# Retention on x without its norm, contiguous mixer weights, and routing tables moved out of two early places for down matrices

## The reference

```python
h = rmsnorm(x, norm_mix_g[0]);  x = x + retention_mixer(h, ...)      # layer 0
h = rmsnorm(x, norm_mix_g[1]);  x = x + conformer_conv_mixer(h, ...) # layer 1
# after each mixer: h = rmsnorm(x, norm_ffn_g[i]); x = x + hierarchical_moe(h, ...)
# retention, per head (4 heads, dk 256, dv 512):
q, k = rotary(h @ w_q), rotary(h @ w_k) * dk ** -0.5;  v = h @ w_v;  g = h @ w_g
o = causal_decayed(q, k) @ v
o = o * rsqrt(mean(o * o) + 1e-6) * head_g
out = (silu(g) * o) @ w_out
# moe: top-1 group of 4, top-2 of its 8 experts, blocks of tokens per expert:
y = (silu(xb @ w_gate[e]) * (xb @ w_up[e])) @ w_down[e]
```

## Time and profile before

| | us |
|---|---|
| median of 3 runs | 1786.35 (1784.78 to 1788.58) |
| the profiled execution | 1786.88 |
| its span | 1785.0 |
| TensorE matmuls, busy | 1471.5 (82%) |
| TensorE weight loads, busy | 936.2 (52%) |
| VectorE busy | 522.5 (29%) |
| ScalarE busy | 486.3 (27%) |
| GpSimd busy | 337.2 (19%) |
| moved by DMA | 473.19 MB, mean 265 GB/s |

### The profile page before, as it was taken

One profiled execution on the slowest core, in us unless ns is written; L12 is line 12 of the kernel. 1 busy time (PEld: TensorE's weight loads), 2 busy tenths in 40 slices (PEclk: granted clock), 3 DMA queues, 4 the chain that ended last, 5 costly groups with the idle time before them and its releaser, 6 DMA issues. The chain is left out here.

```text
span 1785.0 us, 37105 instructions
## 1 busy us (share of the span) xinstructions
PE 1471.5 (82%) x15156; PEld 936.2 (52%) x15157; DVE 522.5 (29%) x1245; ACT 486.3 (27%) x875; POOL 337.2 (19%) x294
## 2 busy tenths in 40 slices
PE   5999999999786889867785899869788878679883
PEld 4878678786443445434353785337344444345442
DVE  3222111212521112111123399961412111112124
ACT  4232422323321222211122324341322122112222
POOL 2424244342000111100011452012010001001100
PEclk8999999999798999999997899979799899999997
DMA  8222122121599999999998121004499999999985
GB/s 283 96 93 94 48 95 95 47 95 53 192 428 429 427 429 427 429 428 429 429 409 288 47 95 47 0 1 164 180 376 414 406 430 423 429 427 428 415 361 212
DMA packets 65156, 473.19 MB, mean 265 GB/s; under 512 B 6509, under 2 KB 23101, under 8 KB 39506
## 3 DMA queue, kind: packets, MB, share of 16 engines
q1 hardware_dynamic: 60064, 463.55, 63.4%
q0 software_dynamic: 4608, 8.41, 1.2%
q10 hardware_dynamic: 434, 0.51, 0.1%
HBM read 461.94 MB, written 14.68 MB: 267 GB/s over the span
## 5 line engine op out<-in xcount | busy, mean ns | idle before, releaser
L787 PE MATMUL ps<-ring,hgT 128*32 128x256 f32 x6016 | 385.3, 409 | 147.2 <-DMA ring<-w_gu 122.7
L787 PEld LDWEIGHTS ps<-ring,hgT 128*32 128x32 f32 x6016 | 202.5, 116 | 318.0 <-DMA ring<-w_gu 147.8
L431 POOL TENSOR_TENSOR w_lo<-ring,w_hi 128x512 fp32r<-128x512 f32 x176 | 233.0, 1326 | 415.1 <-ACT w_hi L511 415.1
L450 POOL DMA_INDIRECT y_dram<-area_c,idx_s x96 | 94.3, 982 | 788.6 <-ACT area_c L547 768.9
L511 ACT CAST w_hi<-ring 128x512 fp32r<-128x512 f32 x176 | 109.1, 625 | 367.1 <-PE ps L692 366.7
L730 PE MATMUL ps<-area_a,block_rows 128*32 128x256 f32 x3136 | 201.3, 400 | 8.9 <-DVE block_rows L976 8.9
L1098 DVE TENSOR_TENSOR a_e<-sg_e,ps 128x128 f32<-128x128 f32 x94 | 27.1, 288 | 613.3 <-ACT sg_e L542 613.3
L803 PE MATMUL ps<-ring,aT_e 128*32 128x256 f32 x2752 | 166.3, 382 | 23.6 <-DMA ring<-w_down 10.7
L730 PEld LDWEIGHTS ps<-area_a,block_rows 128*32 128x32 f32 x3136 | 110.3, 117 | 85.0 <-issue 26.6
L1237 DVE SCALAR_TENSOR_TENSOR area_c<-area_b,par,area_c 128x512 f32<-128x512 f32 x168 | 135.6, 878 | 1.1
L690 PE MATMUL ps<-w_hi,hT_hi 128*128 128x512 f32 x320 | 126.7, 396 | 7.2 <-DVE hT_lo L1262 7.2
(11 more groups left out here) (183 smaller groups left out, 1473.6 us busy)
## 6 DMA issues: line engine op xcount, KB each, us to landing
ring<-w_gu SPq DMA_DIRECT2D x128, 2048.0 KB
ring<-w_down SPq DMA_DIRECT2D x58, 2048.0 KB
ring<-w_in SPq DMA_DIRECT2D x8, 2048.0 KB
ring<-w_in SPq DMA_DIRECT2D x8, 1024.0 KB
ring<-w_out SPq DMA_DIRECT2D x4, 2048.0 KB
ring<-w_pw SPq DMA_DIRECT2D x8, 1024.0 KB
hT<-w_down SPq DMA_DIRECT2D x2, 2048.0 KB, 7.7
area_c<-w_down SPq DMA_DIRECT2D x2, 2048.0 KB, 8.0
```

Source lines behind the costliest of these rows:

```text
L431: nc.gpsimd.tensor_tensor(w_lo[:, place, :], ring[:, s, at:at + 512], w_hi[:, place, :].bitcast(F32), ALU.subtract).then_inc(lo_ready, 1)
L450: pool.indirect_dma_start(y_dram[l], bass.IndirectOffsetOnAxis(ap=idx_s[:, b:b + 1].bitcast(U32), axis=0), y_out[:, b, :], None, bounds_ch ...
L787: last = nc.tensor.matmul(ps[32 * g:32 * g + 32, 2, 0:256], hgT[:, n * (KT // 2) + k, :], gate_up[n][:, k, :, g * P:(g + 1) * P], start=(n ...
```

## The change

1. The norm before retention is no longer computed ahead of it. TensorE turns x itself as each tile lands. ScalarE squares x in the first head, between weight tiles 4 and 5, and the scales are applied to v, to the gate's SiLU, and to the epsilon of the head norm. The counters of later norms move down by one.
2. The mixer weights are laid out on the host as places of the ring, and each is one contiguous load of 2 MB. Router weights and biases are loaded by SyncE behind head 0's gate weights, positions behind its q and k weights. The clamps are on VectorE, and the sine is behind weight tile 8. ScalarE's four heads are written out without a loop.
3. The routing's tables move to area_c from column 4096 and to trig. The down matrices for area_c and area_b are loaded ahead of the routing: in layer 0 right behind the first two experts, in layer 1 when the conv mixer has left z (`hTlo_ready`). Since `y_out` is where the tables are, ScalarE waits for `wts_ready` before a layer's blocks.

```diff
-        onehot_r = over("onehot_r", [P, (NT * 2 + 1) * NE], area_b_at, 400)
-        slot_hot_r = over("slot_hot_r", [P, 8, P], area_c_at, 0)
-        block_hot_r = over("block_hot_r", [P, 8, NBLK], area_c_at, 8 * P)
+        route_at = 4096
+        onehot_r = over("onehot_r", [P, (NT * 2 + 1) * NE], area_c_at, route_at + 1152)
+        slot_hot_r = over("slot_hot_r", [P, 8, P], trig_at, 0)
+        block_hot_r = over("block_hot_r", [P, 8, NBLK], area_c_at, route_at)
...
-            sp.dma_start(area_b[:, 0:S].bitcast(I32), pos_in.partition_broadcast(P)).then_inc(pos_loaded, 16)
             sp.dma_start(const[:, :], const_in).then_inc(const_loaded, 16)
             for i in range(NT):
                 sp.dma_start(x[:, i, :], x_in[i * P:(i + 1) * P, :]).then_inc(x_loaded[i], 16)
-            load_head_qk(0)
-            load_columns(1, w_in, KT, 2 * QK, DV)
+            load_slot(0, w_qk[0])
+            sp.dma_start(area_b[:, 0:S].bitcast(I32), pos_in.partition_broadcast(P)).then_inc(pos_loaded, 16)
+            load_slot(1, w_v[0])
             sp.dma_start(decay[:, :, :], decay_in.rearrange("h p s -> p h s")).then_inc(decay_loaded, 16)
-            load_columns(2, w_in, KT, 2 * QK + RV, DV)
-            load_rows(3, w_out, 0, DV)
+            load_slot(2, w_g[0])
+            sp.dma_start(wr[:, :, :, :], w_router).then_inc(router_loaded, 16)
...
+            load_slot(3, w_out[0])
...
+                if l == 0:
+                    load_spare(1)
+                    load_spare(2)
+                sp.wait_ge(logitT_mm[l], 1)
+                load_spare(0)
                 sp.wait_ge(cum_ready[l], 1)
-                for n, left in enumerate((logitT_mm, idx_mm, wts_ready)):
-                    sp.wait_ge(left[l], 1)
-                    sp.dma_start(spare[n], w_down[l, SPARE[n]]) \
-                        .then_inc(spare_loaded[l][n], 16)
                 if l == 1:
+                    sp.wait_ge(idx_mm[l], 1)
                     sp.dma_start(gfin, g_final.partition_broadcast(P)).then_inc(gfin_loaded, 16)
...
-                        load_columns(j, w_pw1, KT, j * 2 * P, 2 * P)
-                        load_columns(j, w_pw1, KT, j * 2 * P + D, 2 * P, at=2 * P)
+                        load_slot(j, w_pw1[j])
...
+                    sp.wait_ge(hTlo_ready, 3 * KT)
+                    for n in (1, 2):
+                        sp.dma_start(spare[n], w_down[1, SPARE[n]]).then_inc(spare_loaded[1][n], 16)
                     sp.wait_ge(lo_ready, split + TILES)
-                    load_expert(0, w_gu0[1, 0])
+                    load_slot(0, w_gu0[1, 0])
...
-            pool.wait_ge(angle_ready, 1)
-            nc.gpsimd.tensor_scalar(sin, ang, PI, -PI, ALU.min, ALU.max).then_inc(trig_arg, 1)
-            nc.gpsimd.tensor_scalar(cos, low, PI, -PI, ALU.min, ALU.max).then_inc(trig_arg, 1)
...
                 total = act.value_load(cum[0:1, NE:NE + 1], min_val=NE, max_val=NBLK - 1)
+                act.wait_ge(wts_ready[l], 1)
                 with act.Fori(0, total) as t:
...
+            for h in range(HEADS):
...
+                split(0, 0, NWT)
+                if h == 0:
                     for i in range(NT):
+                        act.wait_ge(x_loaded[i], 16)
+                        link.sent(nc.scalar.activation(xn[:, i, :], x[:, i, :], ACT.Square,
+                                                       accum_out=x_ss[:, i:i + 1]))
+                    act.wait_ge(pad_zero, 1)
+                    link.wait()
+                    nc.scalar.activation(x_rt, x_ss, ACT.Sqrt, bias=eps, scale=1.0 / D).then_inc(x_root_ready, 1)
+                split(0, NWT, TILES)
+                if h == 0:
+                    act.wait_ge(trig_arg, 2)
+                    nc.scalar.activation(trig[:, :, :], trig[:, :, :], ACT.Sin).then_inc(trig_ready, 1)
...
+                    nc.scalar.activation(v[:, i, :], ps[:, B + i, :], ACT.Copy, scale=x_rstd2[:, i:i + 1]) \
+                        .then_inc(v_ready, 1)
...
+                    nc.scalar.activation(sg[:, i, :], ps[:, A + i, :], ACT.Silu, scale=x_rstd[:, i:i + 1]) \
+                        .then_inc(sg_ready, 1)
...
+                    nc.scalar.activation(rt[:, i:i + 1], ss[:, i:i + 1], ACT.Sqrt, bias=x_eps[:, i:i + 1],
+                                         scale=1.0 / DV).then_inc(oroot_ready, 1)
...
-            turn_norm(0)
+            for i in range(NT):
+                pe.wait_ge(x_loaded[i], 16)
+                for k in range(KT):
+                    last = nc.tensor.transpose(ps[:, k, i * P:(i + 1) * P], x[:, i, k * P:(k + 1) * P], ident)
+                    if i == NT - 1:
+                        last.then_inc(hT_mm, 1)
...
+            dve.wait_ge(par_loaded, 16)
+            norm_lo(0, 0, G_MIX)
+            V.sem_inc(x_added, 8)
             dve.wait_ge(const_loaded, 16)
...
+            dve.wait_ge(x_root_ready, 1)
+            link.done(V.reciprocal(x_rstd, x_rt))
+            V.tensor_scalar(x_eps, x_ss, EPS / D, EPS * EPS, ALU.mult, ALU.add)
+            V.tensor_tensor(x_rstd2, x_rstd, x_rstd, ALU.mult).then_inc(x_scale_ready, 1)
```

More of the change, by code:

```diff
@@ L89, in done, with program @@
         self.wait()
-def program(nc, x_in, pos_in, const_in, decay_in, par_in, w_in, w_out, w_pw1, w_pw2, b_pw2,
+def program(nc, x_in, pos_in, const_in, decay_in, par_in, w_qk, w_v, w_g, w_out, w_pw1, w_pw2, b_pw2,
             w_router, b_router, w_gu0, w_gu1, w_down, g_final, out):
@@ L120, in program @@
         area_c = sb("area_c", [P, 6144])
+        trig_at = next_tensor()
         trig = sb("trig", [P, 2, S])
@@ L167, in program @@
         expert_exp = small[:, 16:20]
+        x_rstd, x_rstd2, x_eps, x_ss, x_rt = (small[:, n:n + 4] for n in range(20, 40, 4))
         xn = area_a[:, :].rearrange("p (i d) -> p i d", i=NT)
@@ L189, in program @@
                  hT[:, 0:4, :].rearrange("p k s -> p (k s)"), hT[:, 4:8, :].rearrange("p k s -> p (k s)")]
[L192 to L202, removed]
+        room = area_c[:, route_at:route_at + GRP * QW]
+        logitsT = area_c[0:NG + NE, route_at:route_at + S]
+        logits = room[:, 512:656].rearrange("p (i e) -> p i e", i=NT)
+        le = room[:, 656:784].rearrange("p (i e) -> p i e", i=NT)
+        eq = room[:, 784:912].rearrange("p (i e) -> p i e", i=NT)
+        block_hot = room[:, 576:1152].rearrange("p (j b) -> p j b", j=8)
+        work = room[:, 1440:1696].rearrange("p (j e) -> p j e", j=8)
+        table = room[:, 1696:1696 + NBLK]
+        group_hot = room[:, 1768:1784].rearrange("p (i g) -> p i g", i=NT)
+        pick, best, second, gate = (room[:, 1784 + 4 * n:1788 + 4 * n] for n in range(4))
+        rank, base = room[:, 1800:1808], room[:, 1808:1816]
+        ranki, blki = room[:, 1816:1824].bitcast(I32), room[:, 1824:1832].bitcast(I32)
+        count, blocks, upto = room[:, 1832:1864].bitcast(I32), room[:, 1864:1896], room[:, 1896:1928]
         spare = [hT[:, :, :].rearrange("p k s -> p (k s)"), area_c[:, 0:SLOT], area_b[:, 0:SLOT]]
         gfin = trig[:, :, :].rearrange("p a s -> p (a s)")
-        block_hot = area_c[:, 3328:3328 + 8 * NBLK].rearrange("p (j b) -> p j b", j=8)
         y_out = area_c[:, 4096:4096 + GRP * QW].rearrange("p (b c) -> p b c", b=GRP)
@@ L217, in program @@
         par_loaded = sem("par_loaded")
+        router_loaded = sem("router_loaded")
         pos_loaded = sem("pos_loaded")
@@ L1276, in _ @@
             combine(1, 4)
-_NAMES = ("x_in", "pos_in", "const_in", "decay_in", "par_in", "w_in", "w_out", "w_pw1", "w_pw2", "b_pw2",
+_NAMES = ("x_in", "pos_in", "const_in", "decay_in", "par_in", "w_qk", "w_v", "w_g", "w_out", "w_pw1", "w_pw2", "b_pw2",
           "w_router", "b_router", "w_gu0", "w_gu1", "w_down", "g_final")
@@ L1320, with slots @@
                           columns(a["conv_ln_b"]), taps], axis=1)
+    w_in = a["ret_w_in"][0]
+    def slots(w):
+        n = w.shape[1]
+        return w.reshape(KT, P, n, 512).transpose(2, 1, 0, 3).reshape(n, P, SLOT)
     def tiled(w):
```

171 lines of the change are left out of this document (76 added, 95 removed).

## The result

The changed kernel took 1765.94 us (median of four runs, 1763.18 to 1768.34) against 1786.02 us for the kernel before in the same rounds: ratio 0.9886, 95% interval 0.9871 to 0.9902. The forecast was 1769.3 in a range of 1765 to 1777. A repeat of the changed kernel gave 1767.37 (ratio 0.9898, interval 0.9884 to 0.9912). The first median lies 0.9 us inside the forecast's lower edge, the repeat's 2.4. The profiled execution took 1768.34 us with a span of 1766.5, 18.5 us less than the profiled one of before.

A forecast was written before the change was run, and what follows sets the result against it. It took TensorE and ScalarE to bound the mixers and DMA the MoE layers. Terms 8.0 + 7.7 + 0 + 1.8 - 0.2 = 17.3 us gave 1769.6, or 1769.1 against the median; it said 1769.3, range 1765 to 1777.

The forecast's parts named there:

- Start: Kernel start: with the norm off the path and x landing earlier, the first mixer matmul comes 8.0 us earlier.
- the cover: First head: ready matmuls hide ScalarE's squares, root and table load before cast 5; cost nothing, 3 us without it.
- Rival (b): Start: bound by first weights or by a table load before hi copies; 3 to 4 us instead of 8; chance 0.12.
- Mixer: Retention mixer: scale operands cost nothing or hundredths of a microsecond, unrolled ScalarE heads 0, bounds -2 to +1 us.
- Rival (d): ScalarE's four unrolled heads must be fetched, at 80 instructions; 0.22 us each cancels the gain; chance 0.05.
- Stream of the first MoE layer: First MoE layer: spares load before the routing, so slot 0's refill meets an empty queue; 7.7 us earlier.
- rival (a): First MoE layer: stream's shift lost as TensorE becomes the bound near its end; gain left 9.6, 1777; chance 0.10.
- rival (e): Whole change: spares load when they did and x lands as late; about 1785; chance 0.02.
- Second layer: Second MoE layer: early spares bring forward a transfer already hidden; 0 us, bounds -0.3 and +0.3.
- The wait for the weights: Each MoE layer: ScalarE waits for VectorE's last weight before the first SiLU; 0.1 us each, bounds 0 and 1.3.
- Contiguous w_pw1: End of first MoE layer: contiguous conv weights finish before the last scatter; gain 1.8 us, bounds 0.3 and 2.3.
- rival (c): w_pw1 loads: 1 KB runs cost nothing, 352 GB/s comes from scatters beside; last term falls, 1771; chance 0.05.

The follow-up runs named there:

- router_front: Changed kernel with router weights, biases and positions loaded ahead of x again; 1769.33 us, ratio 0.991.
- norm_kept2: Kernel before, norm kept, with contiguous mixer weights and first loads ordered positions, x, then router weights; 1780.65 us, ratio 0.9973.
- norm_kept: Kernel before, norm kept, with contiguous mixer weights and the changed kernel's order of first loads (positions behind w_qk); 1790.74 us, ratio 1.003.
- preload: Changed kernel plus a four-element ScalarE copy ahead of its first wait on data, bringing in the hi copies' table; 1767.13 us, ratio 0.9895.
- dve_order: Changed kernel with the angles ahead of the low parts of x in VectorE's program; 1777.69 us, ratio 0.9957.
- tables: Kernel before with only the third part: routing tables moved, two spare down matrices loaded early, new wait for routing weights; 1777.65 us, ratio 0.9955.
- late0: Changed kernel with layer 0's down matrices for area_c and area_b loaded behind the routing again; 1772.41 us, ratio 0.9929.
- late1: Changed kernel with layer 1's down matrices for area_c and area_b loaded behind the routing again; 1767.03 us, ratio 0.9895.
- best: Changed kernel with an early four-element ScalarE table-load copy and the wts_ready wait moved to the first y_out write; 1766.85 us, ratio 0.9895.
- pw1_strided: Changed kernel with w_pw1 loaded by eight strided loads with 1 KB runs again; 1766.21 us, ratio 0.989.

## Why the prediction was right, and where its steps were off

**Start: 8.0 forecast, 8.64 at the first matmul.** That the sum came out is in part luck, since two of its steps were wrong by nearly the same amount and in opposite directions. By the prediction: x 1.5 us earlier, norm chain 5.66, table load 1.28, in all 8.4. By the trace: x 8.95 - 5.59 = 3.36 earlier, norm chain 5.66 as forecast, transposes to hi copies 7.28 instead of 5.46 (-1.82), hi copies to the first matmul 6.65 instead of 8.09 (+1.44). The first failed term is the rate: 0.58 MB left the queue and gave 3.36 us, or 173 GB/s, where I had assumed at least the 297 GB/s of a full window. `router_front` gives the same price (3.7 us), and positions alone explain most of it: x lands at 8.01 with them ahead (`norm_kept2`) and at 5.68 without (`norm_kept`), 2.3 us for 256 KB. The second is the stretch before the hi copies: 1.29 of the 1.82 is the table load, which I took as gone, and 0.53 the transposes, which take 6.66 us instead of 6.13. I had looked only at the place where the load stood. In the kernel before, the last work ahead of the hi copies was the sine, which brought in its table in the shadow of the transposes, and the copies ran with that:

```profile
17.13 1.28 ACT L562 ACT_TABLE_LOAD   x1
```

With the norm and the sine both moved away, the copies are ScalarE's first work and need a load of their own. I had the case as a bound (1.3 us); `preload` shows that it was this bound that held. Cast 5 started at 25.40, right behind ScalarE's own chain and 5.9 us after the first matmul instead of 5.4, with TensorE busy throughout: the cover held. Rival (b) falls in its first half: the weights had landed by 15.42 at the latest (`preload`). Its second half, the table load, came true and cost its 1.3 us, but not the start. The 8.64 is one pair of executions: with this start unchanged, the first matmul stood at 19.02 to 19.52 in five executions, and with that of before at 27.58 and 28.16, so the gain lies between 8.1 and 9.1. And the order of VectorE's program, which the prediction did not name as a condition, is one: `dve_order` and `norm_kept` lost 10.1 and 8.1 us at the first matmul by it.

**Mixer: 0 forecast, -0.3.** SiLU with a scale operand takes 2.42 us for four instead of 2.07, between products that did not move. Rival (d), straight code that has to be fetched, needed 0.22 us at each of 80 places to cancel the gain, 17.6 in all; the whole mixer lost 0.34, and even that is within what it varies by: 424.5 to 426.7 us from the first product to place 5's load in the nine executions with the new mixer, 424.8 to 425.6 in the four with the old.

**Stream of the first MoE layer: 7.7 forecast, 8.1.** The hole, the empty queue, and the refill were as forecast. The 8.1 has two parts. The refill is issued 2.15 us after the first gate/up matmul instead of 3.56, which gives 1.4, and from there to the last scatter the layer takes 464.0 us instead of 470.7, which gives 6.7 for the two matrices that no longer stand ahead. The shift held to the layer's end, so rival (a) falls. `tables` shows it alone, `late0` takes it away, and since x and the spares land earlier, rival (e) falls too. (Two readings in the prediction were too broad, without effect on the sum: slice 22 moved 288 GB/s, and the second MoE layer's slices 30 to 39 are not flat but lie between 361 and 430.)

**Second layer: 0 forecast, +0.1, and `late1` shows no loss.** The wait for the weights, 0.1 a layer forecast, costs 0.0: the table load now follows it, but the first SiLU starts 3.73 and 3.72 us after the gate/up matmuls, as before. In layer 0 TensorE still releases it (483.73, row above), in layer 1 it follows the load directly (1265.20) and is just in time. `best`, without that wait ahead of the load, ends no earlier.

**Contiguous w_pw1: 1.8 forecast, 1.95 in the stretch** (4.28 to 2.33). The Trainium skill's rule (DMA: Bandwidth & Descriptors, the opening table), by which runs of 512 B reach line rate, does not hold here: 346 to 354 GB/s with 1 KB runs against 427 without, in the same place. The 346 is a window in which no scatter was issued, so rival (c) falls by the rates; the time of `pw1_strided` alone would not have decided it.

**Sum.** 8.3 + 8.1 + 1.95 + 0.1 = 18.45, and the profiled executions differ by 18.5. The medians differ by 20.1 (the ratio's interval is 17.5 to 23.0 us), those of the repeat and the kernel before in the same rounds by 1785.38 - 1767.37 = 18.0 (15.7 to 20.7). Both intervals hold the 18.5 of the trace; whether the times contain a microsecond more is open.

## What to carry to other kernels

When an operation is taken off the path, list what else it did for those behind it (the activation table it brought in, the wait it absorbed), and check each engine's program order for a wait that the moved load now feeds. A transfer is worth moving only where the queue is empty before a refill is due and full after it: the same edit gave 8.1 us in one layer and nothing in the other. Where an edit is worth less than the stages vary, read its own stretch in both traces, since the total can't decide.

## What the runs showed of the hardware

**A small broadcast load at the front is dear.** 256 KB of positions, 2 KB broadcast to 128 rows, delayed the first x tile by 2.3 us, about 110 GB/s, while a full queue of 16 KB rows moves 427 to 430. Whether the short rows, the broadcast or the start of the queue costs it was not separated.

**VectorE slows to GpSimd's pace beside its subtractions.** VectorE's 128x512 step takes 0.43 us where GpSimd is idle (norm_kept), and 1.40 us beside GpSimd's subtractions of 1.3 to 1.4 us each. First row from `norm_kept`, the other two from the changed kernel:

```profile
17.18 0.43 DVE L1112 TENSOR_SCALAR area_c<-area_c 128x512 f32<-128x512 f32 x1
```

```profile
21.21 1.40 DVE L1143 TENSOR_SCALAR area_c<-area_c 128x512 f32<-128x512 f32 x1
...
18.20 5.55 POOL L434 TENSOR_TENSOR w_lo<-ring,w_hi 128x512 fp32r<-128x512 f32 x4 [17.78 <-ACT w_hi L510]
```

The angles take 11.8 us in the changed kernel (with the two clamps in them) against 5.7 in `norm_kept`. In the changed kernel they lie beside TensorE's products and hold up nothing. GpSimd itself loses little: its four subtractions take 5.55 us here and 5.21 before. The Trainium skill (SBUF — State Buffer, on the shared port pair) describes this as a lock held for a whole instruction, and the pace of one VectorE step for each subtraction agrees.

**Stages vary.** Layer 0 from its first refill to its last scatter took 463.7 to 464.1 us in eight executions with early spares and 465.7 in the ninth, the repeat of the changed kernel; from the y loads to layer 1's first refill it was 329.7 to 331.2, and from there to the last y loads 461.5 to 463.5, in kernels whose code there is the same. What sets this was not found.
